# A routed expert layer on Trainium2: expert tokens sent and their rows fetched back through a DRAM buffer by indirect DMAs, instead of one-hot products on TensorE

## The reference

```python
logits = xf @ w_router + b_router                  # 256 tokens, 8 experts
top_val, top_idx = lax.top_k(logits, 2)
gates = jax.nn.softmax(top_val, axis=-1)
# for every expert e: the tokens that chose it
y = (silu(x_e @ we_gate[e]) * (x_e @ we_up[e])) @ we_down[e]     # 1024 -> 2816 -> 1024
out[token] += gate * y[its row]
x = layer_norm(ALPHA * x + (1 + g2) * out, ...)
```

## Time and profile before

| | |
|---|---|
| median of 3 runs | 1275.66 us (1272.66 to 1276.19) |
| span of the profiled execution (first to last instruction) | 1270.9 us |
| the profiled execution's own time | not given apart from its span |
| PE busy | 1183.0 us, 93% |
| DVE busy / ACT busy / POOL busy | 569.0 / 302.1 / 43.8 us |
| DMA bytes | 403.60 MB, mean 318 GB/s |

### The profile page before, as it was taken

The page is one execution under the profiler, slowest core; times in us unless marked ns, Lnnn a source line. Parts: engine busy times, 40 slices in busy tenths (PEclk is TensorE's granted clock), DMA queues, the critical chain, the costliest instruction groups (busy, mean ns, idle before and its releaser), DMA issues.

```text
span 1270.9 us, 26228 instructions
## 1 busy us (share of the span) xinstructions
PE 1183.0 (93%) x11180; PEld 641.1 (50%) x11180; DVE 569.0 (45%) x913; ACT 302.1 (24%) x521; POOL 43.8 (3%) x84
## 2 busy tenths in 40 slices
PE   1889889999999898799999999999999999999996
PEld 1879867788878787523334323334233233333332
DVE  6799988677758999421021020111210210210224
ACT  0557243433336571310010010100100100100100
POOL 2101010000011010000000000000000000000001
PEclk9899989999999999799999999999999999999998
DMA  9973868899727648889999989999989999999950
GB/s 340 312 257 116 290 227 312 322 347 329 244 68 239 201 167 315 334 326 371 413 364 414 394 299 414 412 364 411 388 310 411 410 364 404 396 362 411 379 233 34
DMA packets 149083, 403.60 MB, mean 318 GB/s; under 512 B 19964, under 2 KB 71328, under 8 KB 137696
## 3 DMA queue, kind: packets, MB, share of 16 engines
q1 hardware_dynamic: 146720, 395.16, 82.5%
q0 software_dynamic: 2240, 6.68, 1.4%
HBM read 400.75 MB, written 1.05 MB: 316 GB/s over the span
## 4 chain that ended last, share of the span: by engine, by line
PE 75%; DVE 13%; DMA 6%; issue 3%; ACT 2%; SPq 1%; POOL 0%; DVEq 0%; ACTq 0%
PE bank L1349 36%; PE bank L1368 18%; PE bank L337 5%; PE bank L339 4%; PE bank L338 4%; DVE mod_acc L1541 3%; DMA raw_u<-in_ffn_w_up_dram 2%; DMA u_raw<-in_w_in_dram 2%; DVE u_low L1552 2%; PE bank L1331 1%; DMA mod_first<-in_w_mod_dram 1%; PE bank L1228 1%; DVE score L1596 1%; PE bank L1339 1%; PE bank L1022 1%
## 5 line engine op out<-in xcount | busy, mean ns | idle before, releaser
L1349 PE MATMUL bank<-raw_w,xg 128*32 128x512 f32 (+1 forms) x4608 | 462.9, 557 | 4.5 <-issue 2.5
L1349 PEld LDWEIGHTS bank<-raw_w,xg 128*32 128x32 f32 x4608 | 147.1, 110 | 304.7 <-issue 304.6
L1368 PE MATMUL bank<-raw_w,heT 128*32 128x512 f32 x2112 | 232.9, 593 | 0.0
L1915 DVE TENSOR_TENSOR he<-he,bank 128x256 f32<-128x256 f32 (+1 forms) x72 | 25.6, 384 | 369.4 <-ACT he L869 369.4
L869 ACT ACTIVATE he<-bank 128x256 f32<-128x256 f32 (+1 forms) x72 | 21.2, 367 | 542.8 <-PE bank L1349 542.8
L1368 PEld LDWEIGHTS bank<-raw_w,heT 128*32 128x32 f32 x2112 | 67.3, 110 | 150.5 <-issue 149.3
L1942 DVE SCALAR_TENSOR_TENSOR ycat<-bank,gate_tab,ycat 128x512 f32<-128x512 f32 x36 | 25.4, 747 | 173.0 <-PE bank L1340 171.1
L1541 DVE SCALAR_TENSOR_TENSOR mod_acc<-mod_row,c_act,mod_acc 128x1024 f32<-128x1024 f32 x70 | 89.8, 1283 | 6.8 <-DVE mod_acc L1541 0.9
L337 PE MATMUL bank<-u_high,hT_H 128*128 128x256 f32 x256 | 75.4, 294 | 4.9 <-DVE u_low L1552 3.5
L339 PE MATMUL bank<-u_high,hT_L 128*128 128x256 f32 x256 | 72.8, 284 | 0.0
L338 PE MATMUL bank<-u_low,hT_H 128*128 128x256 f32 x256 | 72.6, 284 | 0.0
(11 more groups left out here) (284 smaller groups left out, 1378.7 us busy)
## 6 DMA issues: line engine op xcount, KB each, us to landing
raw_w<-in_moe_w_down_dram SPq DMA_DIRECT2D x88, 1024.0 KB, 8.6
raw_w<-in_moe_w_gate_dram SPq DMA_DIRECT2D x128, 512.0 KB, 8.5
raw_w<-in_moe_w_up_dram SPq DMA_DIRECT2D x128, 512.0 KB, 9.8
mod_row<-in_w_mod_dram SPq DMA_DIRECT2D x80, 512.0 KB, 6.4
raw_w<-in_moe_w_gate_dram SPq DMA_DIRECT2D x64, 384.0 KB, 5.6
raw_w<-in_moe_w_up_dram SPq DMA_DIRECT2D x64, 384.0 KB, 6.8
u_raw<-in_w_in_dram SPq DMA_DIRECT2D x20, 1024.0 KB, 7.5
raw_d<-in_ffn_w_down_dram SPq DMA_DIRECT2D x11, 1024.0 KB, 10.1
```

Of the source, the lines that this page charges most:

```text
L1349: last = mm(bank[g][32 * q:32 * q + 32, 0:2 * HALF[c]].rearrange("s (m j r) -> s m j r", m=2, r=64), xg[:, i, k, 32 * g:32 * g + 32], cols ...
L1368: last = mm(bank[3 + g][32 * q:32 * q + 32, :], heT[(par + c) % 2][:, g, 2 * a + b, :], W[:, b, h * 512:(h + 1) * 512], start=(c == 0 and ...
L1915: V.tensor_tensor(h, h, bank[g][:, w:2 * w].rearrange("s (j c b) -> s j b c", b=2, c=32), ALU.mult).then_inc(s["m_hid"], 1)
```

## The change

Tokens of the first two experts are still picked on PE, but from unsplit float32 rows `xb`, so with half as many products, each a float32 one. For every later expert the way is by DRAM: a buffer `slots` has 96 rows for each expert number. GpSimd clears it early (24 transfers of 384 KB, 12 in the first mixer and 12 in the dense layer). After the routing, DVE works out the row of each token's two copies (`row_to`), and GpSimd sends the token rows there by four indirect DMAs of 512 KB. ACT loads an expert's 96 rows as `x_rows` by four DMAs of 96 KB (runs of 1 KB), one expert and a half ahead, and DVE turns them in 32x32 blocks into `xg` (`turn_tokens`). That block transpose takes the rows in another order, so SP loads gate and up weights in that order too: partition p of tile k is row 8p + k, where before it was row 128k + p. The runs stay at 4 KB; the distance from one to the next goes from 11,264 to 90,112 bytes.

Each expert's result `y_sum` is written by ACT to the same buffer in one DMA of 384 KB. When all but the last expert's rows are there, GpSimd fetches each token's two rows by four indirect DMAs of 512 KB (`back`), and DVE weighs and adds them. One-hots per expert, their transposes, the products of `scatter`, the split into high and low parts and the additions per expert are gone. The last expert keeps its own path.

```diff
-                    rows = slice(k * P, (k + 1) * P)
-                    sp.dma_start(raw_w[i][:, 0, 0:CHUNK_W[c]], mg[e, rows, f]).then_inc(m_ld[i], 16)
+                    sp.dma_start(raw_w[i][:, 0, 0:CHUNK_W[c]], mg[e, :, f].rearrange("(p b) f -> b p f", b=KT)[k]).then_inc(m_ld[i], 16)
...
+            def clear_slots(first, end):
+                for E in range(first, end):
+                    rows = slice((E + 1) * SLOTS, (E + 2) * SLOTS)
+                    pool.dma_start(slots[rows, :].rearrange("r (a c) -> r a c", a=4),
+                                   zeros[0:SLOTS, :].unsqueeze(1).broadcast_to([SLOTS, 4, 256])).then_inc(s["zeroed"], 16)
...
+                if l == 0:
+                    pool.wait_ge(s["lg_ps"], 2)
+                    clear_slots(0, PASSES * NE // 2)
...
+            pool.wait_ge(s["f_gu"], 2 * STEPS - 6)
+            clear_slots(PASSES * NE // 2, PASSES * NE)
...
+            pool.wait_ge(s["row_to"], 1)
+            for j in range(2):
+                for t in range(TT):
+                    pool.indirect_dma_start(slots[:, :], bass.IndirectOffsetOnAxis(ap=row_to[:, j, t:t + 1], axis=0), xb[t][:], None)\
+                        .then_inc(s["sent"], 16)
...
+            pool.wait_ge(s["y_all"], 1)
+            for t in range(TT):
+                for j in range(2):
+                    pool.indirect_dma_start(back[t][j][:], None, slots[:, :], bass.IndirectOffsetOnAxis(ap=row_back[:, j, t:t + 1], axis=0))\
+                        .then_inc(s["came"], 16)
...
                 act.wait_ge(s["m_y1"], E + 1)
-                for h in range(2):
-                    cc = slice(h * 512, h * 512 + 512)
-                    A(yH[0:SLOTS, cc], y_sum[0:SLOTS, cc], ACT.Copy).then_inc(s["m_yH"], 1)
+                act.dma_start(slots[bass.ds(E * SLOTS, SLOTS), :], y_sum[0:SLOTS, :]).then_inc(s["y_kept"], 16)
+            def load_tokens(E):
+                act.wait_ge(s["x_turned"], E + 1)
+                rows = slots[bass.ds(E * SLOTS + 3 * SLOTS, SLOTS), :].rearrange("(g s) (q c) -> q s g c", g=GROUPS, q=4)
+                for q in range(4):
+                    act.dma_start(x_rows[32 * q:32 * q + 32, :, :], rows[q]).then_inc(s["x_rows"], 16)
...
-                            if cc == 1 and k == 1:
-                                pe.wait_ge(s["m_acc"], E * 4 + 4)
-                                slot_transposes(E)
-                            if cc == 1 and k == 4:
-                                pe.wait_ge(s["m_S"], E + 1)
-                                pe.wait_ge(s["m_yL"], E * 2 + 2)
-                                scatter(0, 6)
-                                scatter(1, 7)
-                            if cc == 2 and k == 2:
-                                pe.wait_ge(s["m_acc"], E * 4 + 6)
-                                scatter(2, 6)
-                                scatter(3, 7)
...
+            def turn_tokens(E, par):
+                dve.wait_ge(s["x_rows"], E * 64 + 64)
+                for g in range(GROUPS):
+                    last = V.transpose(xg[:, par, g].rearrange("p k n -> p (k n)"), x_rows[:, g, :].rearrange("p (f b) -> p b f", b=KT))
...
+            dve.wait_ge(s["came"], 32 * TT)
             for t in range(TT):
+                link(V.tensor_scalar(ycat[:, t, :], back[t][0][:], gate_back[:, 0, t:t + 1], None, ALU.mult))
+                link(V.scalar_tensor_tensor(out=ycat[:, t, :], in0=back[t][1][:], scalar=gate_back[:, 1, t:t + 1], in1=ycat[:, t, :],
+                                            op0=ALU.mult, op1=ALU.add))
```

More of the change, by code:

```diff
@@ L240, in hybrid_decoder @@
         top[0] = end
-        one_G = place("one_G", [P, TT, SLOTS])
-        one_S = place("one_S", [P, T], F32R)
+        zeros = place("zeros", [P, 256])
+        routed = place("routed", [P, 2, TT, NE])
+        row_f = place("row_f", [P, 6, 2, TT])
+        row_to = place("row_to", [P, 2, TT], I32)
+        row_back = place("row_back", [P, 2, TT], I32)
+        gate_back = place("gate_back", [P, 2, TT])
         rank_tab = place("rank_tab", [P, TT, PASSES * NE + 1])
@@ L908, in act_expert @@
                 expert_rows(E, pr, par * PER_EXPERT)
-                slots_of_tokens(E)
+                if not final:
+                    load_tokens(E)
                 silu_chunk(pr, par, 1)
+                if ends:
+                    act.wait_ge(s["y_kept"], E * 16 + 32)
+                    A(tick[:, 3:4], tick[:, 0:1], ACT.Copy).then_inc(s["y_all"], 1)
                 silu_chunk(pr, par, 2)
-                if par and not final:
-                    for r in range(4):
-                        gathered(pr * 4 + 4, r)
                 if not ends:
@@ L1323, in _, with gather @@
             mm4(bank[7][:, 32:40], ones[:, 0:P], sel[:, 1, :], start=False, stop=True).then_inc(s["rank_ps"], 1)
[L1325 removed]
+            def gather(r, b):
                 for i in range(2):
[L1328 to L1340 removed]
+                    for t in range(TT):
+                        last = mm(bank[b][:, i * 2 * SLOTS:(i + 1) * 2 * SLOTS], xb[t][:].rearrange("p (f b) -> p b f", b=KT)[:, 2 * r + i, :],
+                                  one_P[:, t].rearrange("p i n -> p (i n)"), start=(t == 0), stop=(t == TT - 1))
+                last.then_inc(s["xg_ps"], 1)
             def gate_up_tile(pr, n, k, c, i, ends=False):
@@ L1830, in _ @@
             dve.wait_ge(s["small_ld"], 32)
-            lg, cand, oh1, lg2, oh2, tmp, gate = rt[0], rt[1], rt[2], rt[3], rt[4], rt[5], rt[6]
+            lg, cand, base, lg2, tmp, gate = rt[0], rt[1], rt[2], rt[3], rt[5], rt[6]
+            oh1, oh2 = routed[:, 0], routed[:, 1]
             rank, sel, rank_m = rt[7], rt[8], rt[9]
@@ L1871, in _ @@
             link(V.tensor_reduce(npass_f[:, 0:1], bank[7][:, 32:40], AX.X, ALU.max))
-            def one_hot(col, signal):
-                for t in range(TT):
-                    last = V.tensor_scalar(one_G[:, t, :], slot_id[:, 0:SLOTS], rank_tab[:, t, bass.ds(col, 1)], None, ALU.is_equal)
-                last.then_inc(s[signal], 1)
             def pair_one_hot(col):
@@ L1882, in _ @@
             pair_one_hot(1)
-            for i in range(1, 4):
-                last = low_x(i)
-            last.then_inc(s["xsplitL"], 2)
             link(V.tensor_scalar(npass_f[:, 1:2], npass_f[:, 0:1], float(SLOTS), 1.0, ALU.is_gt, ALU.add))
@@ L1902, in _, with both @@
                 last = V.tensor_tensor(gate_tab[:, :, 1 + p * NE:1 + (p + 1) * NE], gate[:], tmp[:], ALU.add)
+            def both(v):
+                return v.unsqueeze(1).broadcast_to([P, 2, TT, NE])
+            at, of, more, other, spare, turn = [row_f[:, i] for i in range(6)]
+            pick = cols[:, 0:4 * NE].rearrange("p (j t e) -> p j t e", j=2, t=TT)
+            link(V.scalar_tensor_tensor(out=base[:], in0=rev, scalar=-float(SLOTS), in1=rank[:], op0=ALU.mult, op1=ALU.add))
+            link(V.tensor_tensor(pick, routed[:], both(base[:]), ALU.mult))
+            link(V.tensor_reduce(at, pick, AX.X, ALU.add))
+            link(V.tensor_tensor(pick, routed[:], both(rank[:]), ALU.mult))
+            link(V.tensor_reduce(of, pick, AX.X, ALU.add))
+            link(V.tensor_scalar(at, at, float(NE * SLOTS + SLOTS - 1), None, ALU.add))
+            for p in range(1, PASSES):
+                link(V.tensor_scalar(more, of, float(p * SLOTS), float(NE * SLOTS - SLOTS), ALU.is_gt, ALU.mult))
+                link(V.tensor_tensor(at, at, more, ALU.add))
+            V.tensor_copy(row_to[:], at).then_inc(s["row_to"], 1)
+            link(V.tensor_scalar(npass_f[:, 3:4], npass_f[:, 1:2], float(NE * SLOTS), None, ALU.mult))
+            link(V.tensor_scalar(other, at, npass_f[:, 3:4], None, ALU.is_ge))
+            link(V.tensor_tensor(turn[:, 0, :], at[:, 1, :], at[:, 0, :], ALU.subtract))
+            link(V.tensor_scalar(turn[:, 1, :], turn[:, 0, :], -1.0, None, ALU.mult))
+            link(V.tensor_tensor(turn, turn, other, ALU.mult))
+            link(V.tensor_tensor(turn, turn, at, ALU.add))
+            V.tensor_copy(row_back[:], turn).then_inc(s["row_back"], 1)
+            link(V.tensor_scalar(spare, other, -1.0, 1.0, ALU.mult, ALU.add))
+            V.tensor_tensor(gate_back[:], v2[:, 0:2, :], spare, ALU.mult)
             norm_out(2)
```

136 lines of the change are left out of this document (50 added, 86 removed).

## The result

The changed kernel takes **1262.49 us** (median of 4 runs, 1259.29 to 1265.18) against 1274.16 us (4 runs, 1271.98 to 1276.19) beside it: ratio 0.9905, 95% interval 0.9888 to 0.9921. It is faster, as predicted, but by 12 us where the sum had 37.6, and it ends just outside the range (1262). The profiled span is 1260.3 us; the sum of the prediction had 1233.3. So 27.0 us have to be found.

The account below looks back on a forecast made before the run. The prediction took PE as the bound, with the weight queue almost level. Span 1270.9 - 37.4 (PE's detours) - 0.2 (first gather) = 1233.3 us, with the median 4.8 above, so 1238 us; range 1231 to 1262 us.

Parts of the forecast that it names:

- PE's loss of work (37.4 us): Routed layer: one-hot transposes, scatter products and later pairs' gathers leave PE's path, 22.9 + 14.5 us gained.
- the gap at the loop's end: End of each routed-layer loop turn: the issue gap of 1.30 us was taken to stay.
- The first gather: First two experts' tokens on PE: starts about 2.0 us earlier, takes 7.6 us instead of 5.84; 0.2 us gained.
- ACT's issues: Five DMAs per expert ahead of silu: 5 us at most, covered by 15.44 us of idle time; counted 0.
- DVE's passes: Kernel's end: four more passes over 128x1024, some 5 us, covered by DVE's 10.9 us wait for PE; counted 0.
- PE's new wait: Ahead of an expert's first down tile: its rows are ready a whole chunk (20.60 us) earlier; counted 0.
- The clears at 0: First mixer and dense layer: GpSimd's 24 clears fit idle issue time and free queue time; counted 0.
- the second twelve: Clears from 308 us: 6.4 us of transfers pushed on, but PE's buffers are loaded a step ahead; 0, otherwise 6.4.
- Rival 3: Clears delay dense layer or first mixer (6.4 us), or ACT's issues wait (8 x 2); 1245 to 1254 us, chance 0.09.
- The weight queue: After 528 us: weights and other transfers need 660 us of some 684, so PE stays the bound.
- the reserve of 10 to 15 us: Routed layer: queue time left from 24 us after early losses, about 3% of gate and up time.
- rival 1: Routed layer: PE becomes queue-bound, gate and up at 380 GB/s, 17 to 22 us lost, about 1258 us; chance 0.20.

Follow-up runs that it names:

- experiment 2: Changed kernel with the first gather reading 128 neighbouring elements instead of steps of 8: 1257.57 us, ratio 0.9878.
- 5: Changed kernel with GpSimd waiting for each clear to land before issuing the next: 1271.53 us, ratio 0.9977.
- 10: Changed kernel with all 24 clears issued in the first mixer at 94.6 us, none in the dense part: 1263.12 us, ratio 0.9904.
- 11: Changed kernel with the 24 clears issued singly over the dense part, tied to PE's finished half steps, none in the first mixer: 1246.89 us, ratio 0.9781.
- experiment 3: Changed kernel with the clears copied from token rows in 4 KB runs instead of zeros in 1 KB runs: 1258.09 us, ratio 0.9874.
- 9: Kernel 7 with the four 16 KB loads issued by SP instead of GpSimd: 1250.47 us, ratio 0.9821.
- experiment 1: Kernel before the change with only the new weight row order and gathers reading tokens to match: 1290.51 us, ratio 1.0126.
- 8: Changed kernel without the four indirect DMAs fetching rows back at the end, token rows used instead: 1257.28 us, ratio 0.9856.
- 7: Changed kernel with all 24 clears as 4 KB-run copies behind the dense part's last gate and up step, last norm's rows loaded later: 1249.0 us, ratio 0.981.
- 12: Kernel 11 with the last norm's two rows loaded behind the experts' last row block: 1245.1 us, ratio 0.9771.

## Why the prediction was off

**PE's loss of work (37.4 us): right.** A turn of the loop takes 170.0 us; before, by the same pieces, it took 181.8 ((1184.66 - 639.21) / 3). That is 11.8 less, of which 10.5 were predicted. The other 1.3, 3.9 us in three turns, are in the main the gap at the loop's end, which I had left standing; it stood at two of the three turns only (1.30 us at 732.04, 1.19 at 914.40). A term missed on the good side.

**The first gather: right in kind, 1.1 us off.** It starts 1.9 us earlier (2.0), and takes 8.61 us, not 7.6. I had named the reading of rows in steps as the way to the upper end of 10.1; experiment 2 prices it at 1.5 us. That 7.6 came near is in part luck: of the two rows it was chosen between, the one at 33 us ran at a granted clock of 0.71 and the one at 173 us at 1.00, which I had not looked at, and the gather itself ran at 0.83.

**ACT's issues, DVE's passes, PE's new wait: hidden, as predicted.** ACT's idle time ahead of silu is 16.99 us at 677.26 (15.44 in the earlier trace rows), and from the last product's start the end takes 17.0 us in both kernels (1243.26 to 1260.3, 1253.91 to 1270.9).

**The clears at 0: the step that failed.** "19 us free of 32; 0" compared bytes with free time over a stretch, and the issue cost with GpSimd's idle time. The issue was even cheaper than reckoned (0.67 us each). But the loads that PE's work hangs on were issued 6.5 us behind twelve clears, and it is the time to land of those four loads that counts, not the mean share of 32 us. It went from 5.3 to 13.0 us, and nothing absorbs it there. For the second twelve I gave 0 with 6.4 us as the other end; 8.8 were measured. "PE there works from buffers loaded a step ahead" was the wrong premise: ACT, which stands between the gate loads and PE, already waited 11.6 us for them before the change, and 19.6 after it. Rival 3 had this mechanism, with 6.4 us for both places together and a chance of 0.09; it came to 19.9. The size of a burst was off too: I reckoned 4.7 MB as 11.5 us of a full queue, at 412 GB/s, and while clears run the queue moves some 290, so they are at least 16 us (19 at the 253 of clears alone). Experiments 5, 10 and 11 show that the cause is the burst, 3 that it is not the form in which the clears are written, 9 that it isn't a matter of one queue.

**The weight queue: right in direction, 10 us off.** PE stayed the bound up to the last expert, but the reserve of 10 to 15 us was used up. It was reckoned from 660 us of transfers at 409 and 425 GB/s, 414 on average. From 600 us on the queue was full and moved 252.85 MB in 622 us, 407 GB/s; at 414 that is 610: some 12 us. (The slow start, 353 GB/s from 548 to 600 us, had been allowed for.) The last norm's two rows, 1.05 MB or 2.5 us, were in no term of the sum, and the shorter turns brought PE 3.9 us closer. Together 18 us, more than the reserve, and PE waited 5.9.

The mis-sized term is the rate of gate and up, 409 GB/s for all of it. It was read where runs of 4 KB pass, but the tiles of the third column chunk (384 KB each) come in runs of 3 KB, not 4 as I had said of the whole. Windows of the changed kernel:

```profile
1104.00:1115.00 11.00, 11.00 (x116) 3.62 (x112) 0.80 (x3) 0.00 (x0) 0.00 (x0) 1.00 1.02 384
675.00:680.00 5.00, 5.00 (x52) 1.54 (x48) 2.09 (x6) 0.94 (x3) 0.00 (x0) 1.00 1.03 400
665.00:675.00 10.00, 10.00 (x100) 3.16 (x96) 0.00 (x0) 0.00 (x0) 0.00 (x0) 1.00 1.05 370
```

In the first two nearly only such tiles pass (the DMA view has all packets but one or none on SP's queue, 4.21 and 2.00 MB in packets of some 3 KB), and the full queue gives 384 and 400; in the third an expert's result and token rows come in between, at 370. The 50.3 MB of these tiles at 384 to 400 instead of 409 GB/s are 3 to 8 us, an estimate; the rest of the 12 would be the expert rows, which were not tested apart. It is a mild case of rival 1, without the loss of rate in the row order that I had looked for: experiment 1 excludes that. The fetch and the norm's rows behind it are a part that was shown by experiments: without the fetch the last expert's stage is 5.4 us shorter, with the rows later 2.6 to 4.5 (8, and 7 and 12).

Two figures of that sum do not come out of its rows: 14 slots of 1.05 MB hold 14.7 MB, not 13.1, and from 528 to 1216 us it is 688 us, not 684. Each would have made the reserve 4 us larger, so they are not why it was used up.

## What to carry to other kernels

A transfer that nobody waits for is not free because the mean share of the queue leaves room: look up which load is issued next behind it and who waits for that, and price the burst as its bytes at the rate it runs at, in that load's landing. If it has no due time, issue it in single pieces tied to PE's progress; here that was worth more than the choice of place, of queue or of run length. And where a change takes PE's detours out of a stage that was level with the weight stream, take the stream's own rate for every size of tile in it, not its best windows, and expect the reserve to end at the last tiles, where here the clock fell behind each longer wait, too.

## What the hardware showed that I had not expected

A stationary operand read in steps of 32 bytes doubled eight float32r products (1.07 to 2.10 us, granted clock 1.00 in both) and added some 1.5 us to sixteen float32 ones (7.15 to 8.61). With nothing but clears on them the DMA engines were full (share 1.02) at only 253 GB/s, or 276 in experiment 3. It is not that writes to DRAM are slow as such: one expert's result of 384 KB among weight loads left the full queue at its rate:

```profile
1089.00:1094.00 5.00, 5.00 (x52) 1.62 (x48) 0.00 (x0) 0.00 (x0) 0.00 (x0) 1.00 1.01 413
```

Why a burst of them is slower was not tested. Weight tiles in runs of 3 KB moved at 384 to 400 GB/s on a full queue, in runs of 4 KB at 409. After waits of 2.33 and 2.91 us PE's granted clock was 0.50 for some 3 us, and the 96 products behind the second took 12.21 us instead of 10.30.
